# Gate spreading: the weights' low halves on DVE instead of POOL, and 64 early tiles instead of 60

## The chip, the cores and the metric
One core of one Trainium2 chip. The metric is the device time of one execution in microseconds. Engines: PE (TensorE), DVE (VectorE), ACT (ScalarE), POOL (GpSimd), SP (SyncE, which issues most DMAs here).

## What is computed
Two blocks over 512 grid tokens and 256 context tokens of width 1024. The change touches only the last part of the second block, a feed-forward layer that picks experts by product keys:

```python
def peer_ffn(u, wq, subkeys, table_u, table_v):
    q = einsum('pd,de->pe', tb, wq)                 # 8 heads, two halves
    s = einsum('phik,hink->phin', q, subkeys)       # 128 keys a half
    s1, i1 = top_k(s[:, :, 0], 16); s2, i2 = top_k(s[:, :, 1], 16)
    top_s, pos = top_k(s1[..., :, None] + s2[..., None, :], 16)
    gate = softmax(top_s)                           # 8 x 16 chosen experts a token
    act = gelu(einsum('pd,phkd->phk', tb, ue))      # ue, ve: rows of the two tables
    return einsum('phk,phkd->pd', gate * act, ve)
```

There are 128 x 128 = 16384 experts. After it come a residual, scaled, and a layer norm.

## The kernel before
The kernel is a sequence of stages. Within a stage each engine runs its own program in order, and semaphores tie them together; a stage ends only when all engines are done.

The layer is `experts` (from route_heads to expert_sums). Tokens are split: for 384 of them (`ND`, three groups of 128) all 16384 experts are computed densely, in 128 tiles of 128 experts, with a gate matrix that is zero where an expert wasn't chosen. For the last 128 tokens the 128 chosen rows of each token are fetched one by one. A tile's first product (tokens with `peer_u`) takes eight steps of three matmuls of 384 columns (`product3`, lines 344 to 346): the fp32 weights are split in a high half, cast by ACT, and a low half, the difference.

Some tiles' first products and Gelus are made early and kept in DRAM (`early_products`): `ROUTE_TILES` = 38 of them beside the routing (`route_heads`), and `EARLY_GROUPS * JG - ROUTE_TILES`, 22, beside the spreading of the gates (`spread_gates`). The last stage, `expert_sums`, reads these E = 60 tiles back, and makes the first products of the other 68 itself.

`spread_gates` turns the routing's lists into the gate matrix. It takes four tokens at a time, called a quad here, 96 quads in all:
- DVE (lines 2426 and 2430) makes the one-hot rows `one` and `two` of four tokens, in a ring of 16 tokens, that is four quads: it waits for `g_done` of the quad four before.
- PE (line 2443) multiplies them, then runs some steps of the early tiles from the generator `stream`. `steps_to(n)` says how many steps stand ahead of quad n: `KD * (count - BEHIND) * n // quads`, so that four tiles (BEHIND) are left for after the last quad.
- ACT (line 2477) copies each quad's product to `gbuf`. In the iteration in which a tile's eight steps are complete it also runs `evict` (Gelu, line 2465) and `high` (the cast, line 2459) for the tile three further on (the ring R is 3).
- POOL (line 2417) makes each tile's low half as soon as its high half is there.
- SP loads the tiles' weights (ring W of 4, freed by `low_ready`), stores the early products, and stores `gbuf` to DRAM in six lots.

The order in ACT is written out by hand:

```python
for n in range(quads):
    act.wait_ge(g_done, n + 1)
    ...
    while done < count and KD * (done + 1) <= steps_to(n):
        evict(done)
        high(done + R)
        done += 1
```

In `expert_sums` the second products (18 matmuls of 512 columns a tile) run for all 128 tiles. For the first E tiles that is all PE has to do; for the others the first products stand between them. DVE makes both low halves (`ul` line 2652, `vl` line 2666, `al` line 2671), the gated products `af` (line 2662), and, for the 128 fetched rows of the other tokens, one dot (line 2637) and one addition (line 2646) each. `rows_before(m)` hands out these rows: one in two tiles up to tile E, the rest spread evenly over the M - E - 4 tiles behind it; the last four tiles have none. A row's dot is in its tile, its addition in the next. POOL only issues the row fetches (line 2555).

Of the kernel before, what the change touches and what calls it, by code (L numbers as in the profile page):

```python
# [16 lines left out]
KD = D // P  # L17
# [10 lines left out]
F32 = mybir.dt.float32  # L28
F32R = mybir.dt.float32r
U32 = mybir.dt.uint32  # L30
ALU = mybir.AluOpType
# [2094 lines left out]
    each(lambda n: dve.max_index(index[n][:, 8:16], best[n][:, 8:16], copy[n]))  # L2126


EARLY_GROUPS = 15
ROUTE_SHARES = (4, 4, 5, 4, 5, 4, 5, 7)  # L2130
ROUTE_TILES = sum(ROUTE_SHARES)
BEHIND = 4
# [229 lines left out]
def spread_gates(core, k, x, chosenT, iota, g_dram, h_dram):  # L2362
# [6 lines left out]
    OH, W, R, BANKS = 16, 4, 3, 3  # L2369
    first, count = ROUTE_TILES, EARLY_GROUPS * JG - ROUTE_TILES  # L2370
    quads, lot = ND // 4, TG // 4
    with ExitStack() as ctx:
        sb = lambda n, s, dt=F32: ctx.enter_context(core.sbuf(n, s, dt))
        w = sb("sg_w", [P, W, KD * P])
        wh, wl = sb("sg_wh", [P, R, KD * P], F32R), sb("sg_wl", [P, R, KD * P], F32R)
# [3 lines left out]
        steps_to = lambda n: KD * (count - BEHIND) * n // quads  # L2379
        with core.stage(f"w_in*{W}", "high_ready", "low_ready", "tile_done", "tile_read", "h_ready", "h_stored*3",  # L2380
# [4 lines left out]
            @block.sync  # L2385
            def _(sp):
                def store(n):
                    if n >= 0:
                        sp.wait_ge(h_ready, n + 1)
                        sp.dma_start(h_dram[first + n], hb[:, n % 3, :]).then_inc(h_stored[n % 3], 16)  # L2390

                def spread(o):
                    sp.wait_ge(g_read, lot * (o + 1))
                    sp.dma_start(g_dram[:, :, o, :].rearrange("g p e -> p g e"),
                                 gbuf[:, o % 2].rearrange("p (g j) t -> p g (j t)", j=JG)).then_inc(g_stored[o % 2], 16)

                done = 0
                for n in range(count + W):
                    if n < count:
                        if n >= W:  # L2400
                            sp.wait_ge(low_ready, n - W + 1)
                        m = first + n
                        sp.dma_start(w[:, n % W, :], d["peer_u"][m // JG, m % JG].rearrange("p k c -> p (k c)")).then_inc(w_in[n % W], 16)
                    store(n - W)
                    while done < N_DG and steps_to(lot * (done + 1)) <= KD * (n - W + 1):
                        spread(done)
                        done += 1
                for b in range(3):
                    sp.wait_ge(h_stored[b], 16 * len(range(b, count, 3)))
                for b in range(2):  # L2410
                    sp.wait_ge(g_stored[b], 16 * (N_DG // 2))

            @block.gpsimd
            def _(pool):
                for n in range(count):
                    pool.wait_ge(high_ready, n + 1)
                    pool.tensor_tensor(wl[:, n % R, :], w[:, n % W, :], wh[:, n % R, :].bitcast(F32),
                                       ALU.subtract).then_inc(low_ready, 1)

            @block.vector  # L2420
            def _(dve):
                for n in range(quads):
                    if n >= OH // 4:
                        dve.wait_ge(g_done, n - OH // 4 + 1)
                    t0 = 4 * n % OH
                    dve.tensor_tensor(one[:, t0:t0 + 4, :], iota.unsqueeze(1).to_broadcast([P, 4, P]),
                                      chosenT[:, 0, 4 * n:4 * n + 4].unsqueeze(2).to_broadcast([P, 4, P]), ALU.is_equal)
                    for a in range(4):
                        t = 4 * n + a
                        ins = dve.tensor_scalar(two[:, t0 + a, :], iota, chosenT[:, 1, t:t + 1], chosenT[:, 2, t:t + 1],  # L2430
                                                ALU.is_equal, ALU.mult)
                    ins.then_inc(hot_ready, 1)

            @block.tensor
            def _(pe):
# [53 lines left out]
def expert_sums(core, k, x, g_dram, h_dram, listed, acc, xs, gate_row, out):  # L2489


    nc, d, ps = core.nc, core.dram, k.ps
    M, E, R, UV = N_JG * JG, EARLY_GROUPS * JG, 3, 5
    x_rows, rows_at, rows_gate = listed
# [209 lines left out]
def experts(core, k, xs, cols, rows, out):  # L2704
    nc, d = core.nc, core.dram
    g_dram = nc.dram_tensor("gates_by_expert", (N_JG, P, N_DG, JG * TG), F32, kind="Internal").ap()
    h_dram = nc.dram_tensor("early_products", (EARLY_GROUPS * JG, P, ND), F32, kind="Internal").ap()
    with ExitStack() as outer:
        xh, xl = (outer.enter_context(core.sbuf(n, [P, KD, NX], F32R)) for n in ("ex_xh", "ex_xl"))
        with ExitStack() as ctx:  # L2710
            sb = lambda n, s: ctx.enter_context(core.sbuf(n, s))
            w, b_rows = sb("mod_w3", [P, 2, KD * 512]), sb("b_rows3", [P, 2, 512])
            norm_turned(core, k, [([xs[:, t, :] for t in range(NXC)], 0, 0)], True, cols[:, 3 * KD:4 * KD, :],
                        cols[:, 2 * KD:3 * KD, :], (xh, xl), k.conds[:, 1], w, rows[:, 2:4, :], b_rows,
                        [d["w_ada_rows"][2 + r] for r in range(2)],
                        None, (b_rows[:], d["b_ada_rows"][2:4].partition_broadcast(P)))
        listed = (outer.enter_context(core.sbuf("x_rows", [P, D])), outer.enter_context(core.sbuf("rows_at", [P, P], U32)),
                  outer.enter_context(core.sbuf("rows_gate", [P, P])))
        with ExitStack() as ctx:
            iota, chosenT = (ctx.enter_context(core.sbuf(n, s)) for n, s in (("iota", [P, P]), ("chosenT", [P, 3, ND])))  # L2720
            load_all(core, [(iota[:], d["iota"].partition_broadcast(P))])
            route_heads(core, k, (xh, xl), iota[:, 0:TOPK], chosenT, h_dram, listed)
            spread_gates(core, k, (xh, xl), chosenT, iota[:], g_dram, h_dram)
        acc = outer.enter_context(core.sbuf("ex_acc", [P, D]))
        expert_sums(core, k, (xh, xl), g_dram, h_dram, listed, acc, xs, rows[:, 2:4, :], out)
# [1233 lines left out]
```

## Time and profile before

| | us |
|---|---|
| median of 3 runs (lowest to highest) | 3914.03 (3913.02 to 3915.43) |
| the profiled execution's own time | 3907.1 |
| its span, at a mean granted clock of 0.952 | 3905.3 |
| gate stage: SP's first load of sg_w at | 2804.8 |
| gate stage: the last Gelu (sg_hb) starts at | 3023.0 |
| last stage: SP's first load at | 3026.9 |
| last stage: tile 60's ex_vl starts at | 3294.65 |

Times in the trace are microseconds from the span's start. In the timeline a row is a run of like instructions on one engine: its start, how long it lasted, the engine, line, operation, output and inputs, and in brackets how long the engine had been idle and what ended that. Matmuls overlap, so their pace is read from start to start. Tile names are given without buffer numbers.

### The profile page before, as it was taken

What the parts mean: (1) busy time and instruction counts of PE and PEld (TensorE: products, weight loads), DVE (VectorE), ACT (ScalarE), POOL (GpSimd) and SP (SyncE); (2) the same over time, 40 slices, a digit from 0 to 9 for tenths busy, and PEclk for the clock granted to TensorE, in tenths of its full rate; (3) what the DMA queues carried; (4) which work ended last, traced back from release to release, by engine and by line L of the source; (5) the groups of instructions that cost most, each with busy time, mean ns of one, the idle gap of its engine ahead of it and who ended that gap; (6) DMA issues with size and microseconds to landing.
All of it is one profiled execution on the core that took longest, in us unless ns stands there. A gap on an engine that the chain in (4) does not pass through costs nothing. (4 is left out here: it accounts for less than half of the span.)

```text
span 3905.3 us, 47836 instructions
## 1 busy us (share of the span) xinstructions
PE 3476.3 (89%) x18212; PEld 2862.4 (73%) x18212; DVE 2490.7 (64%) x4236; ACT 1527.3 (39%) x2531; POOL 765.7 (20%) x457
## 2 busy tenths in 40 slices
PE   7979997997999958888986999799788899999997
PEld 3868886645898857777774554399788688888886
DVE  2547773123887847777774001399997787888787
ACT  3434331104555524555553100333365343444443
POOL 0220010200443311111111110155322111222220
PEclk8979998998999979999998999899899999999999
DMA  5111101331111111111112323233255998898884
GB/s 198 43 33 39 33 17 54 118 152 43 48 46 54 33 39 38 49 44 49 44 39 90 116 81 124 103 135 129 97 196 192 376 356 325 325 327 321 332 329 155
DMA packets 149155, 519.61 MB, mean 133 GB/s; under 512 B 18768, under 2 KB 64704, under 8 KB 127040
## 3 DMA queue, kind: packets, MB, share of 16 engines
q1 hardware_dynamic: 130496, 382.33, 27.9%
q0 software_dynamic: 18432, 134.23, 8.8%
q8 instruction: 146, 2.39, 0.2%
q14 instruction: 81, 0.66, 0.1%
HBM read 473.22 MB, written 43.28 MB: 132 GB/s over the span
## 5 line engine op out<-in xcount | busy, mean ns | idle before, releaser
L344 PE MATMUL ps<-ex_vh,ex_al 128*128 128x512 f32 x768 | 303.3, 395 | 38.0 <-DVE ex_al L2671 38.0
L346 PE MATMUL ps<-ex_vh,ex_ah 128*128 128x512 f32 x768 | 300.9, 392 | 0.0
L345 PE MATMUL ps<-ex_vl,ex_ah 128*128 128x512 f32 x768 | 300.8, 392 | 0.0
L2555 POOL DMA_INDIRECT ex_uv<-in_peer_uv,rows_at x128 | 167.2, 1306 | 650.0 <-DVE ex_acc L2646 602.0
L1848 DVE TENSOR_TENSOR mg_sg<-mg_sg,ps 128x512 f32<-128x512 f32 x32 | 22.0, 687 | 399.1 <-PE ps L1797 364.7
L344 PE MATMUL ps<-hT_high,ma_wl 128*128 128x384 f32 (+1 forms) x576 | 235.9, 410 | 21.3 <-DVE ma_wl L3616 15.2
L344 PE MATMUL ps<-hT_high,hg_wl 128*128 128x384 f32 (+1 forms) x512 | 191.7, 374 | 36.0 <-DVE hg_wl L3088 36.0
L3310 POOL TENSOR_TENSOR ma_ce<-ma_ce,ma_c 128x512 f32<-128x512 f32 x64 | 100.3, 1567 | 600.0 <-ACT ma_ce L3514 600.0
L346 PE MATMUL ps<-hT_high,ma_wh 128*128 128x384 f32 (+1 forms) x576 | 209.5, 364 | 0.0
L345 PE MATMUL ps<-hT_low,ma_wh 128*128 128x384 f32 (+1 forms) x576 | 209.3, 363 | 0.0
L344 PEld LDWEIGHTS ps<-ex_vh,ex_al 128*128 128x128 f32 x768 | 144.8, 189 | 78.0 <-issue 34.8
L2226 POOL TENSOR_TENSOR pr_wl<-pr_w,pr_wh 128x1024 fp32r<-128x1024 f32 x54 | 136.8, 2533 | 297.4 <-ACT pr_wh L2284 297.3
L2666 DVE TENSOR_TENSOR ex_vl<-ex_v,ex_vh 128x1024 fp32r<-128x1024 f32 x128 | 156.3, 1221 | 49.8 <-ACT ex_vh L2612 49.8
L345 PE MATMUL ps<-hT_low,hg_wh 128*128 128x384 f32 (+1 forms) x512 | 183.6, 359 | 0.0
L346 PE MATMUL ps<-hT_high,hg_wh 128*128 128x384 f32 (+1 forms) x512 | 182.9, 357 | 0.0
L346 PE MATMUL ps<-ex_xh,ex_uh 128*128 128x384 f32 x544 | 182.7, 336 | 0.0
L344 PE MATMUL ps<-ex_xh,ex_ul 128*128 128x384 f32 x544 | 182.4, 335 | 0.0
L345 PE MATMUL ps<-ex_xl,ex_uh 128*128 128x384 f32 x544 | 182.2, 335 | 0.0
L346 PEld LDWEIGHTS ps<-ex_vh,ex_ah 128*128 128x128 f32 x768 | 144.8, 189 | 30.8
L2601 ACT ACTIVATE ex_dots<-ex_dots 128x1 f32<-128x1 f32 x128 | 26.0, 203 | 359.3 <-DVE ex_dots L2637 359.3
L345 PEld LDWEIGHTS ps<-ex_vl,ex_ah 128*128 128x128 f32 x768 | 144.9, 189 | 28.3
L2646 DVE SCALAR_TENSOR_TENSOR ex_acc<-ex_uv,ex_wts,ex_acc 128x1024 f32<-128x1024 f32 x127 | 162.5, 1280 | 3.9 <-DVE ex_acc L2646 0.5
(549 smaller groups left out, 9685.6 us busy)
## 6 DMA issues: line engine op xcount, KB each, us to landing
ex_v<-in_peer_uv SPq DMA_DIRECT2D x128, 512.0 KB, 5.9
ex_u<-in_peer_u SPq DMA_DIRECT2D x68, 512.0 KB, 6.4
ma_w<-in_w_in_ma SPq DMA_DIRECT2D x48, 512.0 KB, 3.2
gates_by_expert<-sg_gbuf SPq DMA_DIRECT2D x6, 4096.0 KB, 14.9
ex_g<-gates_by_expert SPq DMA_DIRECT2D x32, 768.0 KB, 8.3
hg_w<-in_w_in_hg SPq DMA_DIRECT2D x40, 512.0 KB, 3.2
pr_w<-in_peer_u SPq DMA_DIRECT2D x38, 512.0 KB, 3.7
mg_wg<-in_w_merge SPq DMA_DIRECT2D x16, 1024.0 KB, 5.1
```

Source lines behind the costliest of these rows:

```text
L344: pe.matmul(out, a[1], b[0], start=start, stop=False)
L345: pe.matmul(out, a[0], b[1], start=False, stop=False)
L346: return pe.matmul(out, a[0], b[0], start=False, stop=stop)
L1848: link(dve.tensor_tensor(sg[:, n % 2, a, :], sg[:, n % 2, a, :], ps[:, b + 2 + a, :], ALU.mult))
L2226: pool.tensor_tensor(wl[:, n % R, :], w[:, n % W, :], wh[:, n % R, :].bitcast(F32), ALU.subtract).then_inc(low_ready, 1)
L2555: pool.indirect_dma_start(uv[:, n % UV, :], None, d["peer_uv"], bass.IndirectOffsetOnAxis(ap=rows_at[:, n:n + 1], axis=0)).then_inc(uv_in[ ...
L2601: act.activation(dots[:, n:n + 1], dots[:, n:n + 1], ACT.Gelu).then_inc(act_ready, 1)
L2646: dve.scalar_tensor_tensor(out=acc[:], in0=uv[:, n % UV, D:2 * D], scalar=wts[:, n:n + 1], in1=acc[:], op0=ALU.mult, op1=ALU.add).then_inc ...
L2666: dve.tensor_tensor(vl[:, m % R, :], v[:, m % R, :], vh[:, m % R, :].bitcast(F32), ALU.subtract).then_inc(vl_ready, 1)
L3310: pool.tensor_tensor(ce[:, i % 2], ce[:, i % 2], cT[:, P * c:P * c + P].unsqueeze(1).to_broadcast([P, J, P]), ALU.mult).then_inc(ce_scaled, 1)
```

## The change
DVE makes the low halves of the gate stage. Its function `low` waits for the high half and, from the fourth tile, for the tile three before to be done; `made` counts them, and a low half is put ahead of quad n as long as `KD * (made - 2) <= steps_to(max(n - 2, 0))`; those left over come behind the last quad. POOL's program in this stage goes. EARLY_GROUPS becomes 16: count is 26 instead of 22, steps_to(n) is 176n // 96 instead of 144n // 96, and E in `expert_sums` is 64 instead of 60.

```diff
--- before.py
+++ after.py
@@ -2126,7 +2126,7 @@
     each(lambda n: dve.max_index(index[n][:, 8:16], best[n][:, 8:16], copy[n]))
 
 
-EARLY_GROUPS = 15
+EARLY_GROUPS = 16
 ROUTE_SHARES = (4, 4, 5, 4, 5, 4, 5, 7)
 ROUTE_TILES = sum(ROUTE_SHARES)
 BEHIND = 4
@@ -2410,16 +2410,20 @@
                 for b in range(2):
                     sp.wait_ge(g_stored[b], 16 * (N_DG // 2))
 
-            @block.gpsimd
-            def _(pool):
-                for n in range(count):
-                    pool.wait_ge(high_ready, n + 1)
-                    pool.tensor_tensor(wl[:, n % R, :], w[:, n % W, :], wh[:, n % R, :].bitcast(F32),
-                                       ALU.subtract).then_inc(low_ready, 1)
-
             @block.vector
             def _(dve):
+                def low(n):
+                    dve.wait_ge(high_ready, n + 1)
+                    if n >= R:
+                        dve.wait_ge(tile_done, n - R + 1)
+                    dve.tensor_tensor(wl[:, n % R, :], w[:, n % W, :], wh[:, n % R, :].bitcast(F32),
+                                      ALU.subtract).then_inc(low_ready, 1)
+
+                made = 0
                 for n in range(quads):
+                    while made < count and KD * (made - 2) <= steps_to(max(n - 2, 0)):
+                        low(made)
+                        made += 1
                     if n >= OH // 4:
                         dve.wait_ge(g_done, n - OH // 4 + 1)
                     t0 = 4 * n % OH
@@ -2430,6 +2434,8 @@
                         ins = dve.tensor_scalar(two[:, t0 + a, :], iota, chosenT[:, 1, t:t + 1], chosenT[:, 2, t:t + 1],
                                                 ALU.is_equal, ALU.mult)
                     ins.then_inc(hot_ready, 1)
+                for n in range(made, count):
+                    low(n)
 
             @block.tensor
             def _(pe):
```

## Rows read from the trace of the kernel before

**Rows 1.** The page's busy line: us, share of the span, instructions, by engine.
```profile
PE 3476.3 (89%) x18212; PEld 2862.4 (73%) x18212; DVE 2490.7 (64%) x4236; ACT 1527.3 (39%) x2531; POOL 765.7 (20%) x457
```

**Rows 2.** Windows by stage: stretch, its us, busy us (count) by engine, PEclk, DMA share, GB/s.
```profile
2900.00:3005.00 105.00, 89.53 (x646) 85.31 (x644) 103.99 (x254) 65.91 (x72) 23.98 (x10) 1.00 0.58 190
...
3060.00:3280.00 220.00, 219.60 (x969) 181.61 (x969) 181.76 (x246) 93.16 (x165) 28.28 (x28) 1.00 0.98 363
...
3294.60:3852.90 558.30, 539.59 (x2690) 482.47 (x2690) 447.85 (x550) 227.27 (x452) 133.08 (x94) 1.00 0.87 319
```

**Rows 3.** Timeline in the gate stage, DVE and POOL: start, us, what.
```profile
2899.26 0.68 DVE L2426 TENSOR_TENSOR sg_one<-iota,chosenT 128x512 f32<-128x512 f32 x1
...
2900.89 0.68 DVE L2426 TENSOR_TENSOR sg_one<-iota,chosenT 128x512 f32<-128x512 f32 x1
2901.49 3.32 DVE L2430 TENSOR_SCALAR sg_two<-iota,chosenT 128x128 f32<-128x128 f32 x4
...
2901.77 2.44 POOL L2417 TENSOR_TENSOR sg_wl<-sg_w,sg_wh 128x1024 fp32r<-128x1024 f32 x1 [7.66 <-ACT sg_wh L2459]
```

**Rows 4.** Gate stage: PE's waits (total, times, longest), and a group by line.
```profile
PE ps L2443 <- DVE sg_two L2430: 29.0, 17, 4.1
...
L2417 POOL TENSOR_TENSOR sg_wl<-sg_w,sg_wh 128x1024 fp32r<-128x1024 f32 x22 | 52.7, 2401 | 187.1 <-ACT sg_wh L2459 187.1
```

**Rows 5.** Timeline in the gate stage, PE: the quads' products.
```profile
2904.87 1.16 PE L2443 MATMUL ps<-sg_two,sg_one 128*128 128x128 f32 x8 [1.45 <-DVE sg_two L2430]
...
2908.54 1.05 PE L2443 MATMUL ps<-sg_two,sg_one 128*128 128x128 f32 x8
...
2909.95 1.05 PE L2443 MATMUL ps<-sg_two,sg_one 128*128 128x128 f32 x8
...
2911.88 1.05 PE L2443 MATMUL ps<-sg_two,sg_one 128*128 128x128 f32 x8
```

**Rows 6.** Timeline in the gate stage, ACT and POOL, one tile's high and low half.
```profile
2909.63 1.07 ACT L2477 COPY sg_gbuf<-ps 128x512 f32<-128x512 f32 x1 [0.86 <-PE ps L2443]
...
2911.18 1.05 ACT L2459 CAST sg_wh<-sg_w 128x1024 fp32r<-128x1024 f32 x1 [0.17 <-ACT sg_hb L2465]
...
2912.31 2.37 POOL L2417 TENSOR_TENSOR sg_wl<-sg_w,sg_wh 128x1024 fp32r<-128x1024 f32 x1 [8.09 <-ACT sg_wh L2459]
```

**Rows 7.** Timeline at the gate stage's opening, ACT and PE.
```profile
2811.73 1.04 ACT L2459 CAST sg_wh<-sg_w 128x1024 fp32r<-128x1024 f32 x1 [0.55 <-DMA sg_w<-in_peer_u]
...
2813.76 1.91 PE L2443 MATMUL ps<-sg_two,sg_one 128*128 128x128 f32 x8
...
2817.39 1.34 PE L2443 MATMUL ps<-sg_two,sg_one 128*128 128x128 f32 x8
```

**Rows 8.** Instructions that read sg_wl: ns min/median/max, first and last start.
```profile
L344 PE MATMUL ps<-ex_xh,sg_wl x176: 334/417/689, 2812.6 to 3022.2; 128*128 128x384 f32 x176
```

**Rows 9.** Timeline in the last stage's second part, DVE: ex_vl's starts.
```profile
3302.02 1.22 DVE L2666 TENSOR_TENSOR ex_vl<-ex_v,ex_vh 128x1024 fp32r<-128x1024 f32 x1
3303.15 1.28 DVE L2646 SCALAR_TENSOR_TENSOR ex_acc<-ex_uv,ex_wts,ex_acc 128x1024 f32<-128x1024 f32 x1
...
3310.53 1.22 DVE L2666 TENSOR_TENSOR ex_vl<-ex_v,ex_vh 128x1024 fp32r<-128x1024 f32 x1
...
3319.29 1.22 DVE L2666 TENSOR_TENSOR ex_vl<-ex_v,ex_vh 128x1024 fp32r<-128x1024 f32 x1
...
3432.06 1.22 DVE L2666 TENSOR_TENSOR ex_vl<-ex_v,ex_vh 128x1024 fp32r<-128x1024 f32 x1
...
3441.96 1.22 DVE L2666 TENSOR_TENSOR ex_vl<-ex_v,ex_vh 128x1024 fp32r<-128x1024 f32 x1
```

**Rows 10.** Timeline in earlier stages, PE: matmuls behind two gaps.
```profile
1376.52 1.13 PE L2873 MATMUL ps<-hg_mix 128*128 128x128 f32 x8 [2.42 <-DVE hg_mix L3133]
...
1560.72 0.45 PE L3430 MATMUL ps<-ma_L,ma_xdt 128*64 128x128 f32 x4 [3.99 <-DVE ma_L L3703]
...
1562.33 0.63 PE L345 MATMUL ps<-hT_low,ma_wh 128*128 128x512 f32 x1
```

## The prediction

> **What bounds the kernel now.** I read the page's busy line first: PE carries 89% of the span [rows 1], so a change counts by what it does to PE's stretches. Then the windows by stage, to see what else is full where the change acts. The gate stage (2804.8 to 3023) has DVE busy without a break, 103.99 of 105.00 us between 2900 and 3005, with PE at 89.53; the first part of the last stage has PE at 219.60 of 220.00, and its second part PE at 539.59 of 558.30 with DVE at 447.85 [rows 2].
>
> In the gate stage a "quad" is four tokens: DVE makes one L2426 and four L2430, PE multiplies (L2443), ACT evicts (L2477), and PE adds one or two steps of three matmuls for the early tiles. DVE's time line shows a quad every 1.63 us (2899.26 to 2900.89), except where POOL makes a low half: the POOL operation of 2.44 us stretches DVE's four L2430 from 1.10 to 3.32 us [rows 3]. So each of the 22 POOL operations costs DVE about 2.2 us, and PE waits 29.0 us in all for DVE's rows, 4.1 of it ahead of quad 0 [rows 4]. PE's own pace, when fed, is start to start 1.41 us for a quad with one step (2908.54 to 2909.95) and 1.93 us with two (2909.95 to 2911.88), so a step is 0.52 and the rest 0.89 us; the quad at 2904.87 starts 0.06 us after DVE's stretched one ends (2901.49 + 3.32) [rows 3, 5].
>
> **What the change does to the work.** POOL's 22 operations go, and DVE's stall with them: 22 x 2.2 = 48 us of DVE time. DVE gets 26 low halves instead. The same operation on the same shape is ex_vl in the last stage, whose start to the next start is 1.13 us, taken as 1.14 (3302.02 to 3303.15, duration 1.22 [rows 9]): 26 x 1.14 = 30 us. By throughput alone DVE gains 18 us, and PE takes four tiles more. With 26 tiles the loop runs 22 of them, steps_to(n) = 176n/96 rounded down: 80 quads with two steps and 16 with one, instead of 48 and 48.
>
> **Where the low half stands in DVE's queue.** DVE is in order, and low(m) waits for high_ready. For m of 3 or more, DVE issues it ahead of the first quad n' for which 8(m-2) <= steps_to(n'-2). ACT makes high(m) after evict(m-3), in the first iteration n for which 8(m-2) <= steps_to(n), and that iteration begins by waiting for quad n's product. So n' = n + 2 always: DVE stops ahead of quad n+2 until ACT has copied quad n, run the Gelu and cast the high half. Queued behind that wait are the one-hot rows of quad n+2; PE has only quads n and n+1 to do. The four-quad ring doesn't help, since the wait comes before the rows are made.
>
> The length of that loop stands in the trace. Quad start on PE at 2908.54, ACT's copy at 2909.63, then the Gelu, the cast at 2911.18, the low half at 2912.31: 3.77 us [rows 5, 6]. POOL started it; I take the same for DVE. Then low half 1.14, the quad's five DVE operations 1.70 (2901.49 - 2900.89 plus the unstretched 1.10), hand-over 0.06: quad n+2 starts on PE 6.67 us after quad n. PE alone would take 3.86 for the pair, 3.34 where one of them has one step, which by the numbering is so in 7 of the 21 pairs: mean 3.69. So PE idles 2.98 us per tile, 21 tiles (m = 3 to 23; the last two lows come after the loop, behind four tiles of PE work): 62.6 us. DVE's recovery at 1.63 a quad is faster than PE's 1.93, but what it gains is thrown away at the next low.
>
> **The gate stage, summed.** Opening: the first three lows stand ahead of quad 0. ACT's third cast starts at 2811.73 and takes 1.04, then 0.03 + 1.14 + 1.70 + 0.06: PE's first quad at 2815.7. Its clock is then at 1.2 GHz, as it is for quad 1 of before, 2813.76 to 2817.39, 3.63 us where the same quad takes 1.93 at 2.4 GHz [rows 7]; quads 0 and 1 together cost 2.9 us extra. Loop: 80 x 1.93 + 16 x 1.41 = 177.0. Waits 62.6. Restart after a wait (the L2443 group takes 1.16 instead of 1.05 us [rows 5]): 21 x 0.1 = 2.1. End: four tiles, 32 x 0.52 = 16.6, their lows covered: the last comes about 9 us after the last quad, and PE gets to it after three tiles, over 12 us. 2815.7 + 2.9 + 177.0 + 62.6 + 2.1 + 16.6 = 3076.9. Before, PE's last step starts at 3022.2 and ends at 3022.7 [rows 8]. **Stage: 54.2 us longer.** The same sum for the kernel before, begun at 2813.76 with its own waits (29.0 less 4.1 [rows 4]), gives 3017.5, which is 5 us short: a one-step quad after a stall goes at DVE's 1.63. I keep +5 for the range and not for the value.
>
> Other queues: SP's load of tile n waits for low(n-4), now DVE's, four periods ahead of its use, so some 40 us cover a transfer; its order past the stores doesn't change. POOL's queue is empty in this stage, and its row fetches start only behind the stage's end, so its freedom buys nothing. Four more stores of 192 KB and four loads of 512 KB lie beside PE work; costed at nothing, worth one landing each if that cover went.
>
> **The last stage.** E goes from 60 to 64. Four tiles move from the second part to the first. First part: 969 matmuls in 220 us, 18 a tile at 0.227 us, so 4.09 us a tile with PE full [rows 2]; the four cost 16.4. Second part: tile to tile is read at ex_vl's starts. A tile with one addition and two dots takes 8.51 (3302.02 to 3310.53), with two and one 8.76 (to 3319.29), with two and two 9.90 (3432.06 to 3441.96) [rows 9]; PE needs 18 x 0.227 + 24 x 0.173 (a third of a step) = 8.2, so the chain over DVE and ACT sets the pace. rows_before puts 98 rows on 64 tiles before and 96 on 60 after; counted by its formula the three kinds go from 30, 29, 4 to 24, 23, 12. Gain: 6 x 8.51 + 6 x 8.76 - 8 x 9.90 = 24.4. **Net 8.0 us shorter.** Bounds: 18.6 if the denser rows cost nothing (4 x (8.73 - 4.09), 8.73 being 558.30 / 64 [rows 2]), 0 if row fetches fall behind.
>
> **Sum.** +54.2 - 8.0 = +46.2. The profiled execution's own time is 3907.1 (the span and 1.8 around it), giving 3953; it lies 6.9 under the median of the runs, 3914.03, and against that median the forecast is **3960**.
>
> **Rivals.** (a) *Slower still, by the clock.* PE now idles some 2.8 us in every tile. The trace holds PE at 2.4 GHz behind one gap of 2.42 us, and shows it at 1.2 GHz (0.63 us for a matmul of 512 columns) 1.6 us after the end of a gap of 3.99 [rows 10]. Ours lies nearer the first, and dense work stands between the gaps. If every gap lowered the clock for as long as it was low in the opening of this stage, quad 1's 1.70 us each time, the time would be 21 x 1.70 = 36 higher: 3996. The Trainium skill, "TensorE: Matmul & The Clock Gate", section "HAM oscillation — how this bites in real kernels", describes a loop in which a wait returns with every tile and each tile then starts cold; by it the sum would be this rival's. No row here has the gap repeated at this spacing. Chance 0.10.
>
> (b) *Faster.* The wait is short or absent, because high halves are ready when DVE asks. Then PE runs from 2815.7 without waits: 2815.7 + 2.9 + 177.0 + 16.6 = 3012.2, the stage is 10.5 shorter, the kernel 18.5: 3896. For it speaks DVE's 18 us of relief, and that DVE was the full engine. Against it stands the order n' = n + 2. The point of decision is the time from quad start to low start: at 3.77 it costs 62.6; the net is zero if each wait were 2.2 us shorter, so at about 1.6 us. ACT's copy alone can't start before 1.09. Chance 0.08.
>
> (c) *Little change.* DVE's wait stands, but PE has more to do in it than I count. If half of the idle went (PE finding its steps' work there and DVE recovering within the tile): 3914 + 46 - 31 = 3929. With three quarters gone, 47 us, it is level. Chance 0.06, half of it within 0.2%.
>
> **Numbers.** The likeliest case, 0.76, alone spans 3948 to 3972 (the +5 above, the end of the last stage's bounds at -18.6, and 0.2 us on the loop's 3.77 for each of 21). The range takes in part of (a): 3945 to 3985. A difference of 0.2%, 7.8 us, is about what a measurement of this kernel tells from none. Faster 0.08, same 0.03, slower 0.89.
>
> **What would show it.** DVE's time line should have a wait of 2.5 to 3 us on sg_wh ahead of 21 of the sg_wl; L2443's idle time should rise from 29 to about 60 us; the stretched L2430 should be gone; PE's start to start should be 6.7 us every fourth or fifth quad. The last stage should begin 54 later and be 8 shorter. A wait under 1 us, or a PE that isn't idle at L2443, would make the forecast wrong; a granted clock under 0.95 in the loop would make it (a).

## The result, and the profile after

The changed kernel takes 3990.22 us (median of 4 runs, 3989.15 to 3992.78) against 3914.65 for the kernel before (4 runs): ratio 1.0195, interval 1.0177 to 1.0212, 76 us slower. The forecast was slower, 3960, range 3945 to 3985. Its direction held, and so did the wait that it named; the time is above the range.

The profiled execution has a span of 3991.0 us, 85.7 more than before's. 7.9 of them lie ahead of the gate stage, where the two programs are the same (SP's first load of sg_w at 2812.64 instead of 2804.76), so I compare stages by their own length. The gate stage, from that load to the store of the last early tile (at 3112.16; before at 3023.51), went from 218.8 to 299.5 us: +80.8. From the last stage's first load to the end (3115.67 to 3990.99; before 3026.93 to 3905.31) it went from 878.4 to 875.3: -3.1. Together +77.7.

The window in the gate stage and the one over the last stage's second part (columns as in [rows 2]), of after:

```profile
2900.00:3000.00 100.00, 77.62 (x474) 75.08 (x474) 66.79 (x183) 47.63 (x52) 0.00 (x0) 0.88 0.43 143
3404.60:3938.10 533.50, 506.74 (x2522) 452.12 (x2521) 429.96 (x529) 215.72 (x432) 133.80 (x92) 1.00 0.88 321
```

DVE, which had no gap before, is now busy for two thirds of the time, PE for 78%, and the granted clock is 0.88 where it was 1.00 [rows 2]. No engine is full: that is what a latency loop looks like, in which each engine waits for the next one around a ring. The waits in the stage up to 3100 (total, times, longest), of after, answer to [rows 4]:

```profile
DVE sg_wl L2419 <- ACT sg_wh L2465: 102.7, 24, 8.8
...
PE ps L2449 <- DVE sg_two L2434: 72.2, 22, 13.9
```

PE's 72.2 contain 13.9 ahead of quad 0, so 58 us are in the 21 gaps of the loop. One period in the timeline of after (PE, ACT, DVE), and below it a window (columns as above) behind the gap:

```profile
2920.48 1.05 PE L2449 MATMUL ps<-sg_two,sg_one 128*128 128x128 f32 x8
...
2922.41 1.05 PE L2449 MATMUL ps<-sg_two,sg_one 128*128 128x128 f32 x8
...
2923.11 1.05 ACT L2465 CAST sg_wh<-sg_w 128x1024 fp32r<-128x1024 f32 x1 [0.17 <-ACT sg_hb L2471]
...
2924.19 1.23 DVE L2419 TENSOR_TENSOR sg_wl<-sg_w,sg_wh 128x1024 fp32r<-128x1024 f32 x1 [4.35 <-ACT sg_wh L2465]
...
2925.94 1.11 DVE L2434 TENSOR_SCALAR sg_two<-iota,chosenT 128x128 f32<-128x128 f32 x4
...
2927.10 1.16 PE L2449 MATMUL ps<-sg_two,sg_one 128*128 128x128 f32 x8 [3.12 <-DVE sg_two L2434]
...
2929.72 1.91 PE L2449 MATMUL ps<-sg_two,sg_one 128*128 128x128 f32 x8
...
2932.68 1.05 PE L2449 MATMUL ps<-sg_two,sg_one 128*128 128x128 f32 x8
```

```profile
2928.50:2931.80 3.30, 3.30 (x15) 3.30 (x14) 3.30 (x11) 1.01 (x2) 0.00 (x0) 0.50 1.03 348
```

The first two rows are quads 35 and 36. ACT's cast ends at 2924.16, DVE's low half starts at once, the quad behind it is ready at 2927.05, and PE takes it at 2927.10. Quad 35, whose product ACT waits for, to quad 37 is 6.62 us; the forecast had 6.67. But look at what follows: the next quad comes 2.62 us later, its eight matmuls take 1.91 us instead of 1.05, and the one after it comes another 2.96 us later. The granted clock is 1.00 through the gap and up to 2928.4, 0.50 in the window shown, that is 1.2 GHz, and 1.00 again from 2931.9. It fell like this in 17 of the 21 periods, somewhere between 0.6 us ahead of the gap's end and 1.4 us behind it.

### The profile page after: what moved, and what is told of

Same layout as the page of the kernel before. It is cut to its first block and busy times, and to the rows that moved or that the text cites. A ratio compares the mean times of both kernels' runs of the same rounds, so it can differ in the third digit from the quotient of the medians.

```text
span 3991.0 us, 47871 instructions
## 1 busy us (share of the span) xinstructions
PE 3507.3 (88%) x18212; PEld 2890.3 (72%) x18212; DVE 2476.8 (62%) x4258; ACT 1532.6 (38%) x2531; POOL 720.1 (18%) x435
## 5 line engine op out<-in xcount | busy, mean ns | idle before, releaser
L2449 PE MATMUL ps<-sg_two,sg_one 128*128 128x128 f32 x768 | 120.1, 307 | 72.2 <-DVE sg_two L2434 72.2
L346 PE MATMUL ps<-ex_xh,ex_uh 128*128 128x384 f32 x512 | 172.0, 336 | 0.0
L344 PE MATMUL ps<-ex_xh,ex_ul 128*128 128x384 f32 x512 | 171.7, 335 | 0.0
L345 PE MATMUL ps<-ex_xl,ex_uh 128*128 128x384 f32 x512 | 171.5, 335 | 0.0
L2449 PEld LDWEIGHTS ps<-sg_two,sg_one 128*128 128x128 f32 x768 | 113.7, 218 | 79.8 <-DVE sg_two L2434 79.8
```

The lines of the kernel that those rows point to most:

```text
L344: pe.matmul(out, a[1], b[0], start=start, stop=False)
L345: pe.matmul(out, a[0], b[1], start=False, stop=False)
L346: return pe.matmul(out, a[0], b[0], start=False, stop=stop)
L2449: mm = pe.matmul(ps[:, 3 + n % 5, P * a:P * a + P], one[:, t, :], two[:, t, :], start=True, stop=True)
```

## The experiments

The time of before that stands beside each run was measured with it on the same chip, and the ratios are to that. Stage lengths are from the profiled executions, measured between the same instructions as above.

**The two halves of the change alone.** First POOL's low halves with 64 early tiles:

```diff
 (before)
-EARLY_GROUPS = 15
+EARLY_GROUPS = 16
```

> POOL makes the low halves as before, 64 early tiles: the second half of the change alone. Theory (order and clock: the loss is DVE's wait for the high half two quads after the quad that frees it, and the clock that falls in each gap of PE): no such wait here; DVE pays 26 stalls of 2.2 us instead of 22, the stage is 5 to 10 us longer and the last stage 3 us shorter: 3914 to 3922. Rival (the four early tiles themselves cost the time, by making PE's loop denser): near 3990.

Measured: 3915.44 against 3913.11, ratio 1.0006 (0.9997 to 1.0016). Gate stage 226.9 (+8.2), last stage from its first load 871.3 (-7.0). By themselves the early tiles cost no time; the rival falls.

Then DVE's low halves with 60:

```diff
 (after)
-EARLY_GROUPS = 16
+EARLY_GROUPS = 15
```

> DVE makes the low halves, 60 early tiles: the first half of the change alone. Theory (order and clock): 17 waits instead of 21; between quad n and n+2 6.64 us where PE alone needs 3.34: 17 x 3.3 = 56, 17 to 21 for the clock, 2 to 3 at the opening, against 160 of PE work in the loop: stage 50 us longer, 3961 to 3968. Rival (the four early tiles cost the time): near 3915. Rival (DVE's load alone: 156 + 22 x 1.14 us of work, less than before): 3900 or under.

Measured: 3969.89 against 3913.11, ratio 1.0141 (1.0124 to 1.0158): 55 to 57 us, 2 us above the 3961 to 3968 that were expected. Gate stage 272.6 (+53.9). So DVE's low halves bring a loss without the four tiles, with 17 waits instead of 21. DVE's work alone, which is less than before, would have made it faster: that rival falls too. The two halves don't simply add up: after has 0.0054, or 21 us, more than this run (gate stage +26.9, last stage -7.1), since four more tiles mean four more waits and more steps in a loop that waits.

**The place of the wait.** The low half two quads later in DVE's order:

```diff
 (after)
-                    while made < count and KD * (made - 2) <= steps_to(max(n - 2, 0)):
+                    while made < count and KD * (made - 2) <= steps_to(max(n - 4, 0)):
```

> After, with each low half two quads later in DVE's order (4 instead of 2 behind the quad that frees it). Theory (order): while DVE waits, PE has four quads in hand, 5.8 us or more of work against 2.7 of wait, 1.14 of low half and 1.6 of quad; PE's gaps go, the clock stays up, DVE and PE both need 177 to 185 us for the loop: 3898 to 3910. If only the gaps were the cost and the clock fell for another reason: 3920 to 3930. Rival (DVE's load, whatever the order): 3985 to 3995.

Measured: 3901.99 against 3913.11, ratio 0.9971 (0.996 to 0.9981): 88 us less than after, from one number. Faster than before, too. Gate stage 211.6. Its window, columns as above:

```profile
2900.00:3000.00 100.00, 99.62 (x717) 97.52 (x716) 100.00 (x279) 72.74 (x79) 0.00 (x0) 1.00 0.72 238
```

The same instructions in another order, and now both PE and DVE are full, at a granted clock of 1.00. DVE's load was never the trouble.

With 3 instead of 4:

```diff
 (after)
-                    while made < count and KD * (made - 2) <= steps_to(max(n - 2, 0)):
+                    while made < count and KD * (made - 2) <= steps_to(max(n - 3, 0)):
```

> After, with each low half one quad later in DVE's order (3 instead of 2). Theory (order and clock): from quad n to quad n+3 6.64 us where PE alone needs 5.8 (less where one has one step): a gap of 0.8 to 1.3 us a tile, too short for the clock to fall: 17 to 22 us over the kernel with 4, without its clock loss: 3916 to 3926, clock 1.00 in the loop. Rival (the order acts as a switch: free or not): 3902, or near 3990.

Measured: 3925.07 against 3916.44, ratio 1.0025 (1.0016 to 1.0035): by the ratios 0.0054, or 21 us, over lag 4. The quads in its timeline:

```profile
2872.34 1.16 PE L2449 MATMUL ps<-sg_two,sg_one 128*128 128x128 f32 x8 [1.20 <-DVE sg_two L2434]
2874.38 1.05 PE L2449 MATMUL ps<-sg_two,sg_one 128*128 128x128 f32 x8
...
2878.24 1.05 PE L2449 MATMUL ps<-sg_two,sg_one 128*128 128x128 f32 x8
2881.04 1.16 PE L2449 MATMUL ps<-sg_two,sg_one 128*128 128x128 f32 x8 [1.22 <-DVE sg_two L2434]
```

From 2874.38 to 2881.04 it is 6.66 us again, but over three quads now. PE alone would need 5.27 for these, of which the last has one step, so 1.4 us are lost here, and some 0.9 where all three have two steps. The loop takes as long as in after; what changes is how much PE has in hand. And behind the gap of 1.20 us at 2872.34 the next quad comes 2.04 us later: the clock holds (1.00 in the window 2900 to 3000).

**The clock.** The order of after, with PE's gap filled by matmuls that no one reads, into the bank of the next tile, which that tile overwrites:

```diff
 (after, in PE's loop behind the steps of quad n)
+                    for m in range(3, count):
+                        if KD * (m - 2) <= steps_to(n - 1) and (n < 2 or KD * (m - 2) > steps_to(n - 2)):
+                            if m > 3:
+                                pe.wait_ge(tile_read, m - 3)
+                            for _ in range(14):
+                                pe.matmul(ps[:, (m - 1) % BANKS, 0:ND], x[0][:, 0, 0:P], x[0][:, 0, 0:ND], start=True, stop=True)
```

> After, with 14 matmuls of 384 columns without use in each of PE's gaps (2.4 us of the 2.6), written to a free bank. The order of DVE and ACT is as in after, so the gap stays. Theory (clock): the granted clock in the loop is 1.00 instead of 0.88, PE's quads behind the gap take 1.4 to 1.9 us each again, and 20 to 25 us come back: 3965 to 3970. Rival (quads behind the gap are slow because of DVE or of the restart): 3990 or a little more, with the clock unchanged or up.

Measured: 3963.77 against 3913.11, ratio 1.0133 (1.0116 to 1.015): 0.0062 or 24 us under after. Gate stage 273.8, 25.7 less. Its window and one filled gap:

```profile
2900.00:3000.00 100.00, 96.38 (x652) 93.24 (x651) 74.56 (x204) 53.37 (x57) 0.00 (x0) 1.00 0.53 174
```

```profile
2901.29 2.59 PE L2458 MATMUL ps<-ex_xh 128*128 128x384 f32 x14
2904.06 1.16 PE L2449 MATMUL ps<-sg_two,sg_one 128*128 128x128 f32 x8 [0.18 <-DVE sg_two L2434]
...
2906.12 1.05 PE L2449 MATMUL ps<-sg_two,sg_one 128*128 128x128 f32 x8
...
2908.05 1.05 PE L2449 MATMUL ps<-sg_two,sg_one 128*128 128x128 f32 x8
```

More work on PE, and 24 us less: the useful quads behind the gap come after 2.06 and 1.93 us instead of 2.62 and 2.96. So the clock's fall is a cost of its own, and the gap (still there, since DVE and ACT were left alone) is the other one. What the gap costs without the clock can be read between this run and lag 4, both at a granted clock of 1.00: 273.8 against 211.6 in the gate stage, 62.2 us.

**What four early tiles are worth.** Lag 4 with 60 tiles:

```diff
 (the run with lag 4)
-EARLY_GROUPS = 16
+EARLY_GROUPS = 15
```

> Low halves on DVE with a lag of 4 quads, 60 early tiles instead of 64. DVE's 160 + 19 x 1.2 us bind the loop instead of PE's 177: the gate stage is 0 to 4 us shorter than with 64, the last stage 3 us longer by what the first runs showed: 3899 to 3906, that is the four early tiles are worth nothing measurable. Rival (they bring 8 us, as the prediction had it): 3908 to 3912.

Measured: 3905.09 against 3916.44, ratio 0.9972 (0.9962 to 0.9982), no different from lag 4 with 64 (0.9971). Gate stage 206.8 against 211.6, last stage 881.0 against 873.8. The tiles take 7.2 us off the last stage, near the 8.0 of the prediction, and put 4.8 on the gate stage; the 2 us left are less than these runs can tell. My reason in the expectation, a gain of only 3 in the last stage, was wrong: it set a version with DVE's low halves beside one with POOL's, and what that does to the last stage is seen further below.

**The opening.** The first three low halves ahead of quads 3, 4 and 5:

```diff
 (the run with lag 4)
-                    while made < count and KD * (made - 2) <= steps_to(max(n - 4, 0)):
+                    while made < count and n >= min(made, 2) + 3 and KD * (made - 2) <= steps_to(max(n - 4, 0)):
```

> Lag 4, 64 tiles, and the first three low halves ahead of quads 3, 4 and 5 instead of all ahead of quad 0. Quad 1 should start at 9 us of the stage instead of 14, since it waits for the first low half alone: 4 to 6 us less than with lag 4: 3896 to 3898. Rival (the opening is hidden, since the stage's loop is bound by DVE, which has the same work): 3901 to 3902.

Measured: 3898.88 against 3916.44, ratio 0.9956 (0.994 to 0.9973). Gate stage 204.9, 6.7 less than with lag 4. Quad 0 no longer stands behind three waits for ACT. By the ratios it is 0.0015, or 6 us, under lag 4, and the two intervals (0.9960 to 0.9981 for lag 4) overlap; it is the stage's length that shows the gain. A second time, in another set of runs:

> The fastest version again (lag 4, 64 tiles, the first three low halves ahead of quads 3, 4 and 5), beside the run with POOL's small operations: 3896 to 3901, ratio to before 0.995 to 0.997, first part of the last stage 280.

Measured: 3893.89 against 3912.61, ratio 0.995 (0.9937 to 0.9964). This is 2 us under the 3896 to 3901 that were expected. This version is the one to keep: 17 to 19 us under before, and by the ratios 2.4% under after (1.0195 against 0.995).

And 68 early tiles:

```diff
 (the run with the opening changed)
-EARLY_GROUPS = 16
+EARLY_GROUPS = 17
```

> As the run before, with 68 early tiles. PE's loop has 208 steps instead of 176, 16.6 us more; the last stage gives back 3 (as measured for the four tiles before) to 8 (by counting its tiles' kinds): 3905 to 3912. Rival (moving tiles out of the last stage always pays): 3894 or under.

Measured: 3906.95 against 3916.44, ratio 0.9977 (0.9967 to 0.9986), 0.0021 or 8 us over the 64. Gate stage 225.7 (+20.8), last stage 866.0 (-7.8). Once PE is full in the gate stage, each tile moved there costs more than it saves.

**The last stage's opening.** In the versions with DVE's low halves the part of the last stage from the first ex_vl to that of tile E is 3.0 to 5.3 us longer than with POOL's and as many early tiles (259.1 for 60, 276.8 for 64); with lag 3, which the expectation below leaves out, it is 1.9 (278.7). A small operation on POOL behind every low half, reading nothing that others write:

```diff
 (the run with the opening changed)
+        scrap = sb("sg_scrap", [P, 8 * count])
...
+            @block.gpsimd
+            def _(pool):
+                for n in range(count):
+                    pool.wait_ge(low_ready, n + 1)
+                    pool.tensor_tensor(scrap[:, 8 * n:8 * n + 8], iota[:, 0:8], iota[:, 0:8], ALU.subtract)
```

> The fastest version (lag 4, the first three low halves spread) with one operation of 8 columns on POOL behind every low half, so that POOL isn't idle through the gate stage. In every run with DVE's low halves the last stage's first part was 4 to 5 us longer than with POOL's (263.0 and 264.4 for 60 tiles where before had 259.1; 280.2 to 281.0 for 64 where it had 276.8), and its first row fetch started 1.7 to 2.0 us after SP's first load instead of 0.8. If POOL's idleness is the cause: fetch at 0.8 us, first part at 276 to 277, 3 to 4 us faster than the run beside it. Rival (the order of the first transfers differs for another reason): 280 and no difference.

Measured: 3893.07 against 3912.61, ratio 0.9949 (0.9936 to 0.9963); beside the run without it (0.995) no difference, where 3 to 4 us were expected. In the profile it does what was expected. The first load of SP and the first row fetch of POOL, with the small operations:

```profile
3017.29 0.32 SPq L2544 DMA_DIRECT2D ex_g<-gates_by_expert  x1
...
3018.09 1.12 POOL L2568 DMA_INDIRECT ex_uv<-in_peer_uv,rows_at  x1 [14.11 <-POOLq L70]
```

and without them:

```profile
3016.39 0.32 SPq L2537 DMA_DIRECT2D ex_g<-gates_by_expert  x1
...
3018.13 1.11 POOL L2561 DMA_INDIRECT ex_uv<-in_peer_uv,rows_at  x1 [239.76 <-issue]
```

The fetch follows after 0.80 us instead of 1.74, and the first part is 275.8 instead of 279.8 us. So with POOL idle through the stage its first fetch is issued 1 us later, behind SP's first load of ex_v (at 0.84 us) instead of ahead of it. Beside that the part is 4 us longer, and 3 from the first load to tile 64, in one profile of each version. The late fetch can't be all of it: with lag 3 the fetch is as late, 1.81 us, and from the first load to tile 64 only 1.0 us is lost against POOL's low halves (286.4 and 285.4). In the medians of five runs the gain doesn't show, so it stays open.

## Why the prediction was right, and where it was wrong

**What bounds the kernel, and the work.** Right. POOL's stall of DVE was gone, the low halves took 1.22 us (median 1226 ns), DVE had less to do. The run with lag 4 shows what that relief is worth when nearly nothing waits.

**The place of the low half in DVE's queue.** Right: n' = n + 2, 6.64 us from quad n to quad n + 2, 21 gaps. PE's wait in them was 58 us, where 62.6 less the end of the last matmul ahead (0.17 each) gives 59. Lag 3 and lag 4 then moved it as the same number says: 6.66 us over three quads, and with four three gaps of 0.2 us in the whole loop. One sign came out otherwise: DVE's waits ahead of these 21 low halves were to be 2.5 to 3 us and are 2.7 to 5.8, 4.1 in the mean. The sign gave DVE the wait worked out for PE, 2.98 us, though DVE has less work per tile; the time of the kernel doesn't hang on it.

**The opening.** Right to 0.6 us: PE's first quad stands 11.5 us behind SP's first load, forecast 10.9. Quad 5 came 23.3 us behind it, where the forecast's numbers give 22.9.

**The clock: the step that failed.** The gate stage was summed at 2.4 GHz from quad 2 on, so the clock stood at nothing in the sum, and its fall was put aside as rival (a) with a chance of 0.10. It fell in 17 of 21 periods. Quad 5 to quad 94 took 253.6 us, where the forecast's numbers give 228.7 (89 quads, 15 of one step, 164.0; 62.6 of waits; 2.1 of restarts): 24.9. Quad 94, behind the last gap, took 1.4 more. These 26 us, of which the filled gaps gave back 25.7, are the miss in the stage (80.8 against 54.2); the opening's 0.4 is the rest. The price that (a) named, 36, was too high by 10: the slow stretch was paid in part and in four periods not at all.

The error was in reading [rows 10]. I took the clock to have survived a gap of 2.42 us and not one of 3.99, and put 2.8 nearer the first. But the first was judged by the matmuls right behind it, the second 1.6 us behind its end. Here is what stood behind the first, two windows (columns as in [rows 2]) and the next row of PE:

```profile
1376.52:1377.50 0.98, 0.98 (x8) 0.93 (x8) 0.94 (x3) 0.00 (x0) 0.98 (x2) 1.00 0.00 0
1377.60:1380.20 2.60, 0.04 (x1) 0.00 (x0) 2.45 (x6) 1.06 (x1) 0.97 (x2) 0.50 0.01 3
```

```profile
1380.24 2.05 PE L2873 MATMUL ps<-hg_mix 128*128 128x128 f32 x8 [2.59 <-DVE hg_mix L3133]
```

The granted clock is 1.00 up to 1377.50 and 0.50 from 1377.60, so it fell 1.0 to 1.1 us behind the end of the gap of 2.42 us, as it fell 1.1 to 1.2 us behind the end of the one of 3.99 (1.00 up to 1561.80, 0.50 from 1561.90). The eight matmuls at 1380.24 take 2.05 us instead of 1.13 for that reason: the clock had fallen ahead of their own gap of 2.59. So the row that was read as safe was not. Nor was it this loop's case: there PE had only 1 to 3 us of work between four gaps (2.38, 1.55, 0.65 and 2.42 us), and the trace can't say which of them brought the fall; here there are some 9 us of work between gaps. The Trainium skill, "TensorE: Matmul & The Clock Gate", section "HAM oscillation — how this bites in real kernels", says that a wait which returns with every tile starts every tile cold. Its waits, for a DMA, are of about 3 to 5 us, and ours of 2.6 to 3.1; the trace agrees with it in 17 of 21 periods, at a granted clock of 0.88, and not in the other four. That rival (a)'s 3996 came within 6 us of the result is partly luck: its 10 us too many stand against 5 that the last stage gained less than forecast.

**The last stage.** The kinds of tiles went to 24, 23 and 12 and took 8.54, 8.78 and 9.93 us; the second part went from 558.3 to 533.5, -24.8 where 24.4 was forecast (the bound of 18.6 used 8.73 for 558.30 / 64, which is 8.72). The first part grew by 21.8 instead of 16.4, and by 17.7 with POOL's low halves. So 4 of the 5 us come with the low halves on DVE, and they went away in the one profile with small operations on POOL. "Its freedom buys nothing" was right; by that profile it even costs a little.

**The rivals.** (b), faster, would have been right about the work and needed what lag 4 has. (c) didn't happen. With the likeliest case at 0.76 and a range whose top, 3985, took in only two thirds of (a)'s 36, the price of (a) was worked out and then mostly left outside.

## What to carry to other kernels

When work moves to an in-order engine, write down the loop: which event releases the instruction, how long the chain to it is, and how many units of work the consumer has in hand at that moment. Here 6.64 us over two units was 88 us slower than the same over four, with the same instructions. A gap of 2.6 to 3.1 us that such a loop leaves on TensorE in every period is to be priced twice, once for itself and once for the clock (62 and 26 us here); gaps up to 1.6 us cost only themselves. Filling the gap with useless matmuls tells the two apart. And when a trace is asked whether the clock survived a gap, the granted clock is to be read for some us behind the gap, not the length of the next matmuls alone.

## What was not expected

- The clock's fall: 24 us of the 76, with gaps of 2.6 to 3.1 us every 12 us and dense matmuls in the 9 us between. Gaps of 0.7 and 1.2 us, as often (lag 3), left the clock at 1.00, and so did the 16 gaps of 1.4 to 1.6 us in before.
- The length of the gap alone doesn't tell whether the clock falls. Of after's 14 gaps of 2.6 us 12 lowered it, of its 7 of 3.1 us 5, and of the 17 gaps of 3.1 us with 60 early tiles 12. What decides is open.
- An engine that was idle for a whole stage starts its first DMA 1 us late: POOL's row fetch at 1.7 to 2.0 us behind SP's first load in the versions that give POOL nothing, 0.8 in those that do. Why is open.
- With lag 4 and PE and DVE both full, DVE's low half took 1294 ns (median, up to 1405) instead of 1226; with the opening changed it was 1224. The difference wasn't followed up.
